# Two sparse layers of a two-layer block, the dense work between them done per token tile beside the row fetches

## The chip, the cores and the metric

One NeuronCore of a Trainium2 chip runs the whole program. The metric is the device time of one execution in microseconds (us). The kernel before takes 3065.58 us, the median of 3 runs (3065.04 to 3068.65). All data is fp32.

## What is computed

256 tokens with 1024 features go through two blocks. The first (pooling and windowed attention, a 32-expert layer, a gated embedding) is left alone. The second has two layers. Layer 0 begins with a recurrent unit, layer 1 with stick-breaking attention; each then has a sparse feed-forward layer (PEER) and a gated embedding (PLE). The part that matters:

```python
def peer_ffn(h, w_q, sub_keys, u_tab, v_tab):      # 8 heads, top 16 of 128x128 experts each
    q = xt @ w_q                                   # [T, 8, 2, 128]
    s = einsum('thpd,hpnd->thpn', q, sub_keys)     # 128 scores per half
    sv, si = top_k(s, 16); cand = sv[0][:, None] + sv[1][None, :]
    cv, ci = top_k(cand, 16)                       # 128 experts (eidx) per token
    act = gelu(einsum('cd,ckd->ck', x, u_tab[eidx]))
    return einsum('ck,ckd->cd', softmax(cv) * act, v_tab[eidx])

def per_layer_embed(h, p, g, w_gate, w_proj):
    return h + sigmoid(rms_norm(h, g) @ w_gate) * (p @ w_proj)

# layer 1, attention: k and v from rms_norm(h, kv_norm), q from rms_norm(h, norm_mix), 16 heads of 64
z = q k^T / 8;  A = exp(log_sigmoid(z) + suffix sum over keys of (log_sigmoid(z) - z)), causal
h = h + (A v) @ w_o
```

A query looks at earlier tokens only, so tile 0 (tokens 0 to 127) needs nothing of tile 1. All other steps of the second block after layer 0's recurrent unit are per token. At the end there is one more root-mean-square norm.

## The kernel before, in words

Activations lie feature-major: `xT`, `hT` and `mT` hold for each of 8 feature chunks 128 partitions x 256 tokens. Weights stream on SP's queue through `ring`, 8 slots of 128x1024 (0.524 MB); `load` (L312) waits until the slot's last user is done, and `plan` fixes the order of all chunks. `dense` (L417) takes a chunk's 128x128 blocks as stationary weights and streams 256 tokens; `token_major` (L430) does v the other way round. fp32 matmuls are issued as two instructions each.

`peer` (L711 on PE, L1008 on ACT, L1425 on DVE, L1578 on POOL) runs once per layer. Norm and queries come first, for both tiles. A **unit** is one head of one tile, 16 picks; there are 16 units, 256 **picks** per layer. A pick fetches for each of the 128 tokens of a tile one row of 8 KB, u and v joined, by an indirect DMA of POOL (L1587) into one of `ROWS` = 16 buffers in `big`. DVE then multiplies u with the tokens and sums (L1477), ACT takes gelu (L1031) of a **share** of 4 picks, DVE makes the coefficients (L1484), ACT scales an identity matrix by each (L1039, `DIAGS` = 8 buffers), and PE multiplies this diagonal with v, two halves of 512 columns, into two PSUM banks (L739). That frees the row buffer. DVE finds the expert numbers of unit n+2 in four pieces, one after each share's dots of unit n (`choose`, L1497). So each engine has its order written out by hand:

```python
for n in range(UNITS):
    for g in range(SHARES):
        share_dots(n, g)
        ...
        if n + 2 < UNITS:
            choose(n + 2, g)
        share_coef(n, g)
```

After layer 0's last pick the outputs are transposed and added to `xT` (L750, L1493). Then for both tiles together: `ple` (L675), k (L424), v (L437), q (L424), attention in groups of four heads (L779 to L813; POOL masks the weights at L1597), the output product, and layer 1's norm and queries. Only then does POOL get the first index of layer 1. Layer 1 ends with `ple` and the final norm; one DMA writes the output (L399).

Of the kernel before, what the change touches and what calls it, by code (L numbers as in the profile page):

```python
# [31 lines left out]
P = 128  # L32
T = 256
# [29 lines left out]
ROWS = 16  # L63
# [3 lines left out]
SHARE = 4  # L67
SHARES = PTOP // SHARE
DIAGS = 8
BIG = ROWS * ROW  # L70

# [38 lines left out]
def plan():  # L110

    first, n = {}, 0
    for name, chunks in (
        ("w_in", 16), ("w_pool", 1), ("w_out", 8), ("w_router", 1), ("b_down", 1), ("proj0", 2), ("ple0", 8),
        ("a_x", 8), ("a_y0", 3), ("w_r", 1), ("a_y1", 1), ("w_i", 1), ("a_y2", 4), ("a_out", 8),
        ("wqa0", 8), ("wqb0", 2), ("keysa0", 1), ("wqc0", 6), ("keysb0", 1), ("proj1", 2), ("ple1", 8),
        ("kv", 16), ("bq", 8), ("bo", 8),
        ("wqa1", 8), ("wqb1", 2), ("keysa1", 1), ("wqc1", 6), ("keysb1", 1), ("proj2", 2), ("ple2", 8),
    ):
        first[name] = n  # L120
        n += chunks
    return first

# [28 lines left out]
def program(nc, io, out):  # L152
    first = plan()
    with ExitStack() as ctx:
# [35 lines left out]
        def half(bank, e):  # L190
# [19 lines left out]
            "diags_ready rows_used out_copied out_turned "  # L210
            "q2_ready k2_ready v2_ready z_done z_used spm_ready rc_done arg_ready a_exp w_exp a_ready o_done o_ready "
# [55 lines left out]
        k2, q2, v2 = lru[0], lru[1], lru[2]  # L267
        st = [big[:, 3 * W + k * SPAN:3 * W + (k + 1) * SPAN] for k in range(28)]
# [22 lines left out]
        def tok_bank(tt):  # L291

            return (2, 0)[tt]

        def out_bank(tt):

            return (6, 4)[tt]
# [9 lines left out]
        def _(sync):  # L307
# [76 lines left out]
            for L in range(2):  # L384
                w, keys = io["peer_w_q"][L], io["sub_keys"][L]
                dense(f"wqa{L}", w)
                for c in range(2):
                    load(first[f"wqb{L}"] + c, w[c * P:(c + 1) * P, SLOT:2 * SLOT])
                load(first[f"keysa{L}"], keys[:, 0:SLOT])
                for c in range(2, DT):  # L390
                    load(first[f"wqc{L}"] + c - 2, w[c * P:(c + 1) * P, SLOT:2 * SLOT])
                load(first[f"keysb{L}"], keys[:, SLOT:2 * SLOT])
                ple(L + 1, io["p2"][L], io["ple_w_proj"][L], io["ple_w_gate"][L])
                if L == 0:
                    dense("kv", io["w_kv"], 2)
                    dense("bq", io["b_w_q"])
                    dense("bo", io["b_w_o"])
            sync.wait_ge(S["out_ready"], 8)
            sync.dma_start(out, mT[:, :]).then_inc(S["out_stored"], 16)  # L399
            sync.wait_ge(S["out_stored"], 16)  # L400
# [3 lines left out]
        def _(pe):  # L404
# [24 lines left out]

            def token_major(n, src, ready, at, cols, outs):  # L430

                for c in range(DT):
                    pe.wait_ge(ready, at + c + 1)
                    w = chunk(n + c)
                    for tt in range(TT):
                        for k, o in enumerate(outs[tt]):
                            last = pe.matmul(o, tile(src, c)[:, tt * P:(tt + 1) * P],  # L437
                                             w[:, cols + k * BANK:cols + (k + 1) * BANK],
                                             start=(c == 0), stop=(c == DT - 1), skip_group_check=True)
                    last.then_inc(w_used, 1)  # L440
# [270 lines left out]
            def peer(L, norm, at):  # L711
                sum_squares(norm)
                dense(first[f"wqa{L}"], hsrc, 0, h_ready, at)
                dense(first[f"wqb{L}"], hsrc, 4, cs=range(0, 2))

                def scores(z):
# [941 lines left out]
```

## Time and profile before

| | |
|---|---|
| median of 3 runs | 3065.58 us |
| profiled execution | 3064.01 us, its span 3062.2 us |
| TensorE (PE) busy, mean granted clock | 2637.0 us (86%), 0.937 |
| VectorE (DVE) busy | 1343.3 us (44%) |
| ScalarE (ACT) busy | 544.5 us (18%) |
| GpSimd (POOL) busy | 509.5 us (17%) |
| moved by DMA | 1025.92 MB, mean 335 GB/s |
| of that, indirect row fetches | 540.05 MB |

The span runs from the first to the last instruction. Busy times of engines overlap. A slice of the page is a fortieth of the span, 76.6 us. Layer 0's picks are in slices 19 to 27, the dense part between the layers in 27 to 31, layer 1's picks from 31 to 40. Which engine sets the pace of a stretch is read from who waits for whom there.

### The profile page before, as it was taken

Reading aid. Unit: us, or ns where it says so; the run is one execution under the profiler, and the core shown is the slowest. Engines: PE = TensorE matmul, PEld = TensorE weight load, DVE = VectorE, ACT = ScalarE, POOL = GpSimd, SP = SyncE. Lnnn points to the kernel's source line nnn. Section 1 sums busy time; section 2 is a strip of 40 time slices with the busy share of each in tenths; the row PEclk is TensorE's granted clock in tenths of the full one; section 3 lists DMA queues with packets and bytes.
Section 4 is the critical chain, followed back from the end, with each engine's and each line's share of the span. In section 5 each row is a group of like instructions: output and inputs, shape, how many; then the busy total and the mean of one; then the engine's idle time right before and its main releaser. Section 6 shows DMA issues by size and latency. Waiting matters only on the chain.

```text
span 3062.2 us, 29257 instructions
## 1 busy us (share of the span) xinstructions
PE 2637.0 (86%) x10044; PEld 1391.2 (45%) x10044; DVE 1343.3 (44%) x3484; ACT 544.5 (18%) x1283; POOL 509.5 (17%) x556
## 2 busy tenths in 40 slices
PE   8789999999999998997778777789888778787787
PEld 6554444444443436784333333347677333333335
DVE  2222221212212223416777777641234777777752
ACT  0210010000101002202222222211331222122212
POOL 1000000000000000004333333300012333333320
PEclk9779999999999998998998999999889898989999
DMA  6259999999999993349999999953216999999990
GB/s 216 94 208 417 417 419 417 418 417 418 418 417 419 417 406 113 128 137 393 421 421 422 421 421 421 421 231 123 90 61 256 422 421 421 422 421 422 421 420 34
DMA packets 169837, 1025.92 MB, mean 335 GB/s; under 512 B 17488, under 2 KB 17904, under 8 KB 71184
## 3 DMA queue, kind: packets, MB, share of 16 engines
q0 software_dynamic: 74880, 540.05, 42.5%
q1 hardware_dynamic: 94864, 484.73, 40.1%
q8 instruction: 46, 0.75, 0.1%
q14 instruction: 47, 0.39, 0.0%
HBM read 1022.09 MB, written 2.62 MB: 335 GB/s over the span
## 4 chain that ended last, share of the span: by engine, by line
PE 44%; DMA 36%; DVE 8%; SPq 7%; issue 2%; ACT 2%; POOL 1%; DVEq 0%; ACTq 0%; POOLq 0%
DMA big<-in_uv,small 28%; PE ps L424 12%; PE ps L569 11%; PE ps L739 9%; DMA big<-in_w_gate_up 7%; SPq L342 4%; PE ps L559 3%; SPq L334 2%; PE ps L604 1%; DVE big L1477 1%; PE ps L414 1%; PE ps L437 1%; POOL big L1587 1%; PE ps L683 1%; DMA big<-in_w_down 1%
## 5 line engine op out<-in xcount | busy, mean ns | idle before, releaser
L739 PE MATMUL ps<-big,small 128*128 128x512 f32 x2048 | 1008.1, 650 | 283.8 <-ACT small L1039 283.8
L1587 POOL DMA_INDIRECT big<-in_uv,small x512 | 484.1, 946 | 2174.4 <-DVE small L1466 1406.6
L739 PEld LDWEIGHTS ps<-big,small 128*128 128x128 f32 x2048 | 415.2, 208 | 872.7 <-issue 492.9
L1477 DVE SCALAR_TENSOR_TENSOR big<-big,ps 128x1024 f32<-128x1024 f32 x512 | 617.6, 1219 | 349.6 <-DMA big<-in_uv,small 347.9
L569 PE MATMUL ps<-big 128*64 128x512 f32 x3072 | 705.8, 600 | 24.2 <-DMA big<-in_w_gate_up 21.6
L569 PEld LDWEIGHTS ps<-big 128*64 128x64 f32 x3072 | 202.9, 137 | 421.6 <-issue 333.9
L424 PE MATMUL ps<-hT,ring 128*128 128x256 f32 x1408 | 317.4, 388 | 14.5 <-DVE hT L1126 11.5
L424 PEld LDWEIGHTS ps<-hT,ring 128*128 128x128 f32 x1408 | 272.9, 195 | 58.6 <-DVE hT L1126 13.1
L1039 ACT ACTIVATE small<-con,small 128x128 f32<-128x128 f32 x512 | 163.6, 390 | 293.1 <-DVE small L1484 293.1
L1303 DVE COPY big<-ps 128x512 f32<-128x512 f32 x32 | 22.1, 692 | 426.1 <-PE ps L569 426.1
L1289 DVE TENSOR_TENSOR big<-ps,big 128x256 f32<-128x256 f32 x64 | 27.2, 425 | 308.2 <-PE ps L586 308.2
L1031 ACT ACTIVATE small<-small 128x4 f32<-128x4 f32 x128 | 26.3, 205 | 694.6 <-DVE big L1477 694.6
L559 PEld LDWEIGHTS ps<-small,mT 128*128 128x128 f32 x1024 | 120.0, 196 | 26.6 <-issue 26.6
L559 PE MATMUL ps<-small,mT 128*128 128x64 f32 x1024 | 124.4, 281 | 1.0 <-DVE small L1273 1.0
L424 PE MATMUL ps<-mT,ring 128*128 128x256 f32 x512 | 113.1, 383 | 5.2 <-issue 3.1
L424 PEld LDWEIGHTS ps<-mT,ring 128*128 128x128 f32 x512 | 98.2, 192 | 20.3 <-issue 3.9
L941 ACT COPY big<-ps 128x512 f32<-128x512 f32 x32 | 18.7, 585 | 421.0 <-PE ps L569 421.0
L414 PE MATMUL ps<-mT,con 128*128 128x256 f32 x176 | 48.4, 431 | 25.2 <-ACT mT L845 25.2
L604 PE MATMUL ps<-small,big 64*128 64x256 f32 x512 | 65.4, 396 | 2.4 <-ACT small L928 2.4
L933 ACT ACTIVATE big<-big 128x256 f32<-128x256 f32 x64 | 26.7, 417 | 225.6 <-DVE big L1290 225.6
L604 PEld LDWEIGHTS ps<-small,big 64*128 64x128 f32 x512 | 48.3, 191 | 31.5 <-issue 27.1
L414 PEld LDWEIGHTS ps<-mT,con 128*128 128x128 f32 x176 | 37.2, 218 | 35.5 <-ACT mT L845 21.9
(246 smaller groups left out, 1633.2 us busy)
## 6 DMA issues: line engine op xcount, KB each, us to landing
big<-in_w_gate_up SPq DMA_DIRECT2D x256, 1024.0 KB, 20.5
big<-in_w_down SPq DMA_DIRECT2D x128, 1024.0 KB, 24.2
ring<-in_peer_w_q SPq DMA_DIRECT2D x32, 512.0 KB, 3.7
ring<-in_w_in SPq DMA_DIRECT2D x16, 512.0 KB, 5.2
ring<-in_a_w_in SPq DMA_DIRECT2D x16, 512.0 KB, 3.6
ring<-in_ple_w_gate SPq DMA_DIRECT2D x16, 512.0 KB, 5.9
big<-in_uv,small POOLq DMA_INDIRECT x512, 26.3
ring<-in_w_kv SPq DMA_DIRECT2D x16, 512.0 KB, 3.7
```

The source lines that it names most:

```text
L334: sync.dma_start(moe_slot(k), io["w_gate_up"][e, k * P:(k + 1) * P, :]).then_inc(moe_loaded[k], 16)
L342: sync.dma_start(moe_slot(GU_CHUNKS + k).rearrange("p (s d) -> p s d", s=2), src)\
L414: last = pe.matmul(ps[:, 7, 0:T], ones, tile(mT, c), start=(c == 0), stop=(c == DT - 1))
L424: last = pe.matmul(half(bank, e), w[:, e * P:(e + 1) * P], src(c), start=(c == 0 and e % 2 == 0), stop=(c == DT - 1), skip_group_check=True)
L437: last = pe.matmul(o, tile(src, c)[:, tt * P:(tt + 1) * P], w[:, cols + k * BANK:cols + (k + 1) * BANK], start=(c == 0), stop=(c == DT - 1 ...
L559: last = pe.matmul(ps[:, G_X, c * CAP:(c + 1) * CAP], mT[:, tt * D + c * P:tt * D + (c + 1) * P], m_sel[:, tt * CAP:(tt + 1) * CAP], start ...
L569: last = pe.matmul(ps[side * CAP:(side + 1) * CAP, bank + b, :], o, w[:, at:at + BANK], start=start, stop=stop, skip_group_check=True)
L604: last = pe.matmul(half(G_OUT, side * DT // 2 + c), m_y[at, c * P:(c + 1) * P], m_gateT[at, :], start=False, stop=True, skip_group_check=True)
L739: last = pe.matmul(ps[:, out_bank(tt) + z, :], diagonal(k), rows(k)[:, D + z * BANK:D + (z + 1) * BANK], start=(k % (PH * PTOP) == 0), sto ...
L1039: act.activation(diagonal(k), ident, ACT.Copy, scale=coef[:, k:k + 1])\
L1477: ins = dve.scalar_tensor_tensor(u, u, 1.0, tok, op0=ALU.mult, op1=ALU.mult, accum_out=dots[:, k:k + 1])
L1587: pool.indirect_dma_start(out=rows(k), out_offset=None, in_=io[f"uv{L}"], in_offset=bass.IndirectOffsetOnAxis(ap=rows_at[:, k:k + 1], axis ...
```

## The change

`ROWS` goes from 16 to 10, `SHARE` from 4 to 2. The 512 picks of both layers become one sequence of 4 **phases** of 128 picks (layer 0 tile 0, layer 0 tile 1, layer 1 tile 0, layer 1 tile 1), and a phase has 64 **ticks** of 2 picks. **Chain** q is what follows phase q's picks for that one tile. Chains 0 and 1 hold PLE, k, v, q, attention, output product, and layer 1's queries and scores; chains 2 and 3 hold PLE and the final norm. In each tick of phase f every engine first does its share of the picks and then one step of chain f-1. Chain 3 runs after the last pick, in 9 ticks. The steps sit at fixed ticks:

```diff
-ROWS = 16
+ROWS = 10
-SHARE = 4
+SHARE = 2
+PHASES = 2 * TT
+PHASE = PH * PTOP
+TICKS = PHASE // SHARE
+ADD, PROJ, SQUARE, SCALE, TURN, GAIN, GATE, SIGMOID, GATED = 0, 0, 0, 1, 1, 2, 2, 6, 7
+SQUARE2, SCALE2, TURN2, GAIN2 = 7, 8, 8, 9
+KEY, VALUE, KEY_COPY, KEY_TURN, KEY_KEEP, VALUE_KEEP = 9, 13, 13, 14, 15, 17
+QUERY, QUERY_COPY, QUERY_TURN, QUERY_KEEP = 17, 21, 21, 22
+HEADS, GROUP, GROUPS = 22, 3, HEADS2 // 4
+MERGE, ADD3, SQUARE3, SCALE3, TURN3, GAIN3 = 34, 38, 38, 39, 39, 40
+ASK, ASK_COPY, SCORE, SCORE_KEEP = (40, 44), (44, 48), (44, 48), (45, 49)
+TOKENS, CHOOSE = 49, 46
+TAIL_TICKS = 9
```

The dense products (GATE, KEY, VALUE, QUERY, MERGE, ASK) take 4 ticks each, 2 chunks a tick. The order on PE, and DVE's tick:

```diff
+            for f in range(1, PHASES):
+                if f >= 2:
+                    pe.wait_ge(S["scores_kept"], 4 + 4 * (f - 1))
+                for t in range(TICKS):
+                    picks(f, t)
+                    chain(f - 1, t)
+            for t in range(TAIL_TICKS):
+                chain(3, t)
...
+            def share(f, t):
+                n = f * TICKS + t
...
+                for which, piece in chosen(f, t):
+                    choose(which, piece)
+                at = slice(n * SHARE % PICKS, n * SHARE % PICKS + SHARE)
+                dve.wait_ge(S["gelu_ready"], n + 1)
+                dve.scalar_tensor_tensor(coef[:, at], acts[:, at], p_rec[:, u16:u16 + 1], cv[:, at],
+                                         op0=ALU.mult, op1=ALU.mult).then_inc(S["coef_ready"], 1)
```

In phase 0 a piece of `choose` runs in every second tick, two units ahead. In later phases the phase's own last six units are chosen in ticks 0 to 40, and the next phase's first two units in ticks 46 to 53.

The chain keeps the residual token-major (`xk`, in place of `hT`). A dense product of one tile has the tile's features as stationary operand and streams the weights in two halves of 512 columns; only the queries keep the old form, with 128 tokens streamed. A root-mean-square is one ACT instruction with an accumulator, then a root; the scaled tile is transposed on PE and multiplied by the gain on ACT and DVE:

```diff
+                def stationary(seg, src, bank, cs, begin=0):
+                    for c in cs:
+                        w = chunk(first[f"{seg}{q}"] + begin + c)
+                        for z in range(2):
+                            last = pe.matmul(ps[:, bank + z, :], src[:, blocks(c)], w[:, z * BANK:(z + 1) * BANK],
+                                             start=(c == 0), stop=(c == DT - 1), skip_group_check=True)
+                        last.then_inc(w_used, 1)
...
+                            for e in range(DT):
+                                last = pe.matmul(ps[:, A + e // 4, blocks(e % 4)], w[:, blocks(e)], hd[:, blocks(c)],
+                                                 start=(c == 0 and e % 4 == 0), stop=(c == DT - 1), skip_group_check=True)
+                            last.then_inc(w_used, 1)
```

In the attention a group of four heads takes 3 ticks, on operands of 512 columns in chain 0 and 1024 in chain 1. ACT and DVE (the masks moved from POOL to DVE):

```diff
+                    if t == HEADS + GROUP * g + 1:
+                        act.wait_ge(S["z_done"], no + 1)
...
+                        step.link(act.activation(sides(a_buf, cols), pair(bank, cols), ACT.Abs))
+                        step.link(act.activation(a, a, ACT.Exp, scale=-1.0))
+                        act.activation(a, a, ACT.Ln, bias=1.0).then_inc(S["ln_ready"], 1)
+                    if t == HEADS + GROUP * g + 3:
+                        act.wait_ge(S["arg_ready"], no + 1)
+                        act.activation(w_buf[:, 0:cols], w_buf[:, 0:cols], ACT.Exp).then_inc(S["w_exp"], 1)
...
+                    if t == HEADS + GROUP * g + 4:
+                        dve.wait_ge(S["w_exp"], no + 1)
+                        dve.tensor_tensor(heads(w_buf), heads(w_buf), mask2, ALU.mult).then_inc(S["a_ready"], 1)
```

SP loads the weights of every chain anew, POOL fetches in one loop, and the output leaves in four pieces:

```diff
+            for q in range(TT):
+                ple_chain(q)
+                dense(f"kv{q}", io["w_kv"], 2)
+                dense(f"bq{q}", io["b_w_q"])
+                dense(f"bo{q}", io["b_w_o"])
+                for z in range(2):
+                    for c in range(DT):
+                        load(first[f"ask{z}_{q}"] + c, w[c * P:(c + 1) * P, z * SLOT:(z + 1) * SLOT])
+                    load(first[f"keys{z}_{q}"], keys[:, z * SLOT:(z + 1) * SLOT])
+            sync.wait_ge(w_used, first["bq1"] + 8)
+            sync.dma_start(hd2, io["final_row"].partition_broadcast(P)).then_inc(S["gain_loaded"], 16)
+            for tt in range(TT):
+                ple_chain(TT + tt)
+                for z in range(2):
+                    sync.wait_ge(S["out_ready"], 2 * tt + z + 1)
...
+            for n in range(2 * UNITS):
+                pool.wait_ge(S["idx_ready"], n + 1)
+                for k in range(n * PTOP, (n + 1) * PTOP):
+                    if k >= ROWS:
+                        pool.wait_ge(S["rows_used"], k + 1 - ROWS)
```

## Rows read from the trace of the kernel before

**Rows 1.** The page's second part, 40 slices: DMA busy tenths, then GB/s.

```profile
DMA  6259999999999993349999999953216999999990
GB/s 216 94 208 417 417 419 417 418 417 418 418 417 419 417 406 113 128 137 393 421 421 422 421 421 421 421 231 123 90 61 256 422 421 421 422 421 422 421 420 34
```

**Rows 2.** The page's chain that ended last, its shares by line.

```profile
DMA big<-in_uv,small 28%; PE ps L424 12%; PE ps L569 11%; PE ps L739 9%; DMA big<-in_w_gate_up 7%; SPq L342 4%; PE ps L559 3%; SPq L334 2%; PE ps L604 1%; DVE big L1477 1%; PE ps L414 1%; PE ps L437 1%; POOL big L1587 1%; PE ps L683 1%; DMA big<-in_w_down 1%
```

**Rows 3.** Windows: busy us of each engine, granted PE clock, DMA share, GB/s.

```profile
1700.00:2000.00 300.00, 232.95 (x487) 96.95 (x486) 212.81 (x533) 66.35 (x180) 113.27 (x120) 0.92 1.01 421
2046.00:2339.00 293.00, 264.69 (x1193) 216.48 (x1194) 70.98 (x156) 70.93 (x128) 12.13 (x16) 0.92 0.30 100
2100.00:2186.00 86.00, 84.04 (x317) 61.24 (x315) 6.41 (x14) 3.98 (x8) 0.00 (x0) 0.98 0.43 143
2186.00:2253.00 67.00, 52.06 (x289) 43.97 (x289) 31.84 (x64) 47.38 (x90) 12.13 (x16) 0.77 0.01 5
3003.00:3062.00 59.00, 44.15 (x201) 36.90 (x200) 16.56 (x28) 12.64 (x19) 0.00 (x0) 0.95 0.10 36
```

**Rows 4.** Waits, 1410 to 2000 us: us in total, times, longest.

```profile
POOL big L1587 <- PE ps L739: 371.3, 232, 8.4
...
DVE big L1477 <- DMA big<-in_uv,small: 149.9, 136, 2.7
...
PE ps L739 <- ACT small L1039: 126.7, 52, 5.5
...
DVE small L1484 <- ACT small L1031: 3.8, 5, 2.7
```

**Rows 5.** Line 1587, the row fetches: count and first issue; us from issue to landing.

```profile
L1587 POOL DMA_INDIRECT big<-in_uv,small x512: 932/936/1167, 1382.3 to 2965.6; - x171
...
DMA to landing us min/median/max: 8.3/26.3/33.2
```

**Rows 6.** Chain that ended last, pieces in order: start us, us, what.

```profile
2006.19 30.02 DMA big<-in_uv,small
2036.24 1.24 DVE big L1477 x2
2038.46 7.15 PE ps L739 x16
...
2128.95 27.47 PE ps L437 x64
...
2325.14 3.58 PE ps L722 x32
```

**Rows 7.** The page's sixth part: a load of weights by itself.

```profile
ring<-in_peer_w_q SPq DMA_DIRECT2D x32, 512.0 KB, 3.7
```

**Rows 8.** DMA, 1368 to 1402 us: weight loads beside the first row fetches.

```profile
ring<-in_ple_w_gate SPq DMA_DIRECT2D x6, 512.0 KB, 8.7
```

**Rows 9.** Lines: busy us, mean ns of one; idle before it, releaser.

```profile
L1477 DVE SCALAR_TENSOR_TENSOR big<-big,ps 128x1024 f32<-128x1024 f32 x512 | 617.6, 1219 | 349.6 <-DMA big<-in_uv,small 347.9 <-PE ps L730 1.7
...
L1039 ACT ACTIVATE small<-con,small 128x128 f32<-128x128 f32 x512 | 163.6, 390 | 293.1 <-DVE small L1484 293.1
...
L1031 ACT ACT_TABLE_LOAD x30 | 38.5, 1283 | 0.5
...
L1264 DVE TENSOR_SCALAR small<-small 128x128 f32<-128x128 f32 x64 | 15.4, 283 | 4.7 <-DVE small L1257 4.6
...
L1085 ACT ACTIVATE big<-big 128x384 f32<-128x384 f32 x16 | 8.4, 523 | 0.5
...
L1013 ACT COPY big<-ps 128x512 f32<-128x512 f32 x16 | 8.2, 600 | 103.1 <-PE ps L424 103.1
...
L1132 DVE TENSOR_TENSOR xT<-ps,xT 128x512 f32<-128x512 f32 x12 | 7.5, 683 | 87.9 <-PE ps L424 87.9
```

**Rows 10.** Timeline at the end: start us, us, the output's issue.

```profile
3057.88 0.35 SPq L399 DMA_DIRECT2D out<-mT  x1
```

More of the change, by code:

```diff
@@ L398, in _ @@
-            sync.wait_ge(S["out_ready"], 8)
-            sync.dma_start(out, mT[:, :]).then_inc(S["out_stored"], 16)
-            sync.wait_ge(S["out_stored"], 16)
+            w, keys = io["peer_w_q"][0], io["sub_keys"][0]
+            dense("wqa", w)
+            for c in range(2):
+                load(first["wqb"] + c, w[c * P:(c + 1) * P, SLOT:2 * SLOT])
+            load(first["keysa"], keys[:, 0:SLOT])
+            for c in range(2, DT):
+                load(first["wqc"] + c - 2, w[c * P:(c + 1) * P, SLOT:2 * SLOT])
@@ L428, in dense @@
                         between(c)
[L430 to L440, printed above, removed]
             hsrc = lambda c: tile(hT, c)
@@ new lines, in queries, with keep, exps @@
+            def queries(z):
+                for b in range(4):
+                    act.copy(pq[:, (4 * z + b) * BANK:(4 * z + b + 1) * BANK], ps[:, 4 * z + b, :])\
+                        .then_inc(S["pq_ready"], 1)
+            def keep(z):
+                used_through(act, f"keys{'ab'[z]}", 1)
+                for b in range(2):
+                    act.copy(tile(mT, 2 * z + b, BANK), ps[:, 4 * z + 2 + b, :]).then_inc(S["scores_kept"], 1)
+            def exps(n):
+                act.wait_ge(S["cv_ready"], n + 1)
+                u = n % UNITS
+                e = cv[:, u * PTOP:(u + 1) * PTOP]
+                act.activation(e, e, ACT.Exp, bias=p_nmax[:, u:u + 1], accum_out=p_sum[:, u:u + 1])\
+                    .then_inc(S["cv_exp"], 1)
@@ new lines, in _ @@
+            squares(5)
+            used_through(act, "wqa", 8)
+            queries(0)
+            keep(0)
+            used_through(act, "wqc", 6)
+            queries(1)
+            keep(1)
+            exps(0)
+            exps(1)
+            for f in range(PHASES):
+                for t in range(TICKS):
+                    share(f, t)
+                    for n, piece in chosen(f, t):
+                        if piece == 3:
+                            exps(n)
+                    if f == 0 and t in (6 * SHARES + 1, 7 * SHARES + 1):
+                        tt = t // SHARES - 6
+                        act.wait_ge(S["x_turned"], tt + 1)
+                        for z in range(2):
+                            act.copy(xk[:, tt * D + z * BANK:tt * D + (z + 1) * BANK], ps[:, 4 + z, :])\
+                                .then_inc(S["x_kept"], 1)
+                    if f:
+                        chain(f - 1, t)
@@ L1116, in _ @@
+            for t in range(TAIL_TICKS):
+                chain(3, t)
         @block.vector
@@ L1565, in _ @@
+            norm(5, [("norm_ffn", 0)])
+            for n in range(2):
+                for piece in range(4):
+                    choose(n, piece)
+            for f in range(PHASES):
+                for t in range(TICKS):
+                    share(f, t)
+                    if f:
+                        chain(f - 1, t)
+            for t in range(TAIL_TICKS):
+                chain(3, t)
         @block.gpsimd
```

792 lines of the change are left out of this document (436 added, 356 removed).

## The prediction, made before the changed kernel was run

> **What bounds the kernel now.** I read the page first. The DMA share is 9 tenths over most of the span and falls in four places; two lie around the change, slices 27 to 30 and the very end [rows 1]. The chain that ended last gives 28% of the span to the row fetches [rows 2]. The windows say how. While rows are fetched the 16 DMA engines are full at 421 GB/s, with TensorE (PE) busy 233 of 300 us, VectorE (DVE) 213, ScalarE (ACT) 66; in the 293 us between the two sparse layers they move 100 GB/s and PE is busy 265 us [rows 3]. The waits confirm it: DVE waits for rows and PE for the diagonals that follow from them, while DVE hardly waits for ACT [rows 4]. So the fetches are DMA-bound, the part between is PE-bound, and they never overlap. That is what the change can win; the question is what it pays.
>
> **One row fetch** is 128x8 KB = 1.049 MB, at 421 GB/s 2.49 us. Test: the first issue is at 1382.3 us, the last landing of layer 0 at 2036.2, 653.9 us [rows 5, 6]. The shortest landing, 8.3, plus 256x2.49 = 637.4, plus some 6 weight chunks of 0.524 MB at 1.25 us (7.5), is 653.2. The model holds, and I use it for the change. The Trainium skill ("DMA: Bandwidth & Descriptors", Where 436 GB/s comes from) puts the HBM limit of a core near 358 GB/s; the row at 421 contradicts it, and I go by the row. By the page the added weights below would cost about 30 us more.
>
> **The sum, DMA first.** After the change there are 512 fetches in an unbroken stream: 1274.9 us. Between them run the weights: chain 0 and chain 1 load 60 chunks each (2 projection, 8 gate, 16 key/value, 8 query, 8 output, 16 next queries, 2 keys), chains 2 and 3 load 10 each, and 2 are in before the first fetch: 138x1.25 = 172 us. What was loaded once in the gap, where no rows moved, is now loaded twice and between rows: the price is 172 us for a gap of 293. Gain vector and output are 1 MB, 2 us. With 8.3 at the start the last row lands, if DMA never pauses, at 1382.3+8.3+1274.9+172+2 = 2839.5. Phase 0 is thereby some 320 us, phases 1 and 2 395 each (319+75), phase 3 332.
>
> **PE beside it.** Picks: 233/300 of 319 = 248 us a phase. Chain of one tile: a token-stationary 1024x1024 product was 27.47 us for both tiles, so 13.7 for one [rows 6]. Gate, k, v, q, output are five: 68.5. The next queries keep weights stationary over 128 columns, 256 instructions at 3.58/32 = 0.112 us: 28.6. Scores 3.6, projection 3.4, six transposes of 8 instructions 5.4. Attention was 52 us busy at clock 0.77 for both tiles [rows 3], so 40 at full speed, 20 a tile (less for the first, more for the second). Sum 130: 378 of 395 us. PE stays just under DMA.
>
> **DVE.** 213/300 of 319 = 227. The halved share adds 32 gelu/coefficient steps of 0.4: 13. Chain: ten 512-column operations at 0.69, three scalings at no more than the 1.22 of a dot product over 1024 columns, 16 gains of 128 columns at 0.28, attention 32/2 = 16, and the masks that leave POOL, about 4: 35 us [rows 3, 9]. 275 of 395. **ACT:** 71 + 32x0.2 + attention 47/2, some 24 copies and gains (14), three root-mean-squares at 4 us, and 20 table loads in the attention at 1.28 (26): about 155 [rows 3, 9]. **POOL** loses the masks, keeps its fetches, and no longer waits for them; its order is otherwise the same. **SP** now has the final gain vector and the first tile's output in its queue, ahead of the last chain's weights; those are needed only 60 ticks later, nothing.
>
> **Fewer buffers.** 26.3 us to landing is 10.6 fetches in flight, so 5.4 of 16 were held by compute [rows 5]. With shares of 2 they are held shorter, about 4 of 10, 6 in flight; 8.3/2.49 = 3.3 are enough. Zero; it costs from the point where over 6.7 are held.
>
> **Where ticks are longer than their DMA.** A tick is 2 picks, 5 us of DMA, 7.5 where 2 chunks come along. Dense tick: PE 3.6+3.4 = 7.0, inside. Attention, three ticks a group, 15 us: ACT has 3 gelus and 6 diagonals (3.0), 5 table loads (6.4), and four operations that are 0.52 us at 384 columns, so some 0.6 at 512 (first tile) and 1.0 at 1024 (second), plus a copy: 12 and 14 us. It hands over in line to DVE (argument, mask, coefficients), 5 to 6 us: 17 and 20. Four groups lose 8 and 20, and the top-16 pieces that DVE runs there another 5 for the second tile; 8 chunks are prefetched meanwhile, 10 us of DMA work, so 0 and 15 are left. Table switches around the three root-mean-squares hold DVE about 2 us each, 14 in all, half of it taken up by the buffers: 7. PE at 96% of DMA in order queues a little: 4 us per phase, 8. **Stalls 30 us.** The trace shows no such interleaving, so the bounds: nothing is lost (0); or PE keeps all the idle time that it has beside rows now (67 of 300 us), so that chain work adds to 319 us: 319+130 = 449, 54 more than 395 twice, plus 15 in phase 3: 123. I take 30, near the low end, because what stands idle now waits for rows, not for a neighbour [rows 4].
>
> **Tail.** After the last landing, two dots, gelu, two diagonals and 8 matmuls: 7 us (9.4 before). Then before it was 59 us for both tiles [rows 3]. Now for one: add 1.4, square and root with table 3.2, scale 1.2, transposes and gains 2.4, gate 13.7, sigmoid 1.2, product and sum 2.8, square and root 3.0, final scaling 1.6, output 4.3 [rows 10], hand-overs 1.2: 36.
>
> Span: 2839.5+30+7+36 = 2912.5 against 3062.2. The profiled execution is 1.8 longer than its span, and 1.6 shorter than the median: **2915 us** in terms of the median, 4.9% less.
>
> **Rivals.**
> A. *All stalls are hidden*: the buffers and the prefetched chunks swallow them. For: in the rows DVE waits 150 us for DMA, so there is room. Against: PE at 96%. Gives 2885.
> B. *PE becomes the bound.* Its granted clock in the rows is 0.92 on average, between its levels of 1.2 and 2.4 GHz, against 0.98 in the dense part, since it stands between bursts [rows 3]. If it keeps the gaps as well as the slow stretches: 123 us instead of 30, 3008. If instead the chain fills the gaps and the clock is full, PE needs 228+130 = 358 and the forecast has more room. The Trainium skill ("TensorE: Matmul & The Clock Gate", Whether your matmuls stay warm) sides with the second: activity releases the clock. The trace agrees as far as 0.98 where PE is busy 84 of 86 us; no row shows the mix.
> C. *Ten buffers are too few.* Weight chunks beside row fetches land after 8.7 us instead of 3.7 [rows 7, 8], so the queues share the engines, and row latency rises too. If 7 are held, 3 are in flight, 8.3/3 = 2.77 us a row, 0.28x512 = 143 more: 3058, no change. Against: 4.6 in flight would do even at today's holding.
> D. *Slower: lockstep.* In a chain tick DVE's dots, ACT's gelu, DVE's coefficients, ACT's diagonals, PE's picks and chunks come one after another, and the next tick starts only when a chain wait (keys turned, weights used, spm, arguments) is over, because each engine's program is in order. Serial, a dense tick is 2.3+1.3+0.4+0.8+7.0 = 11.8 instead of 7.5, an attention or hand-over tick 3 more than 5: 2x(28x4.3+22x3) = 373 us, 3258. It decides from 178 us, 1.8 us per tick over 100 ticks. Against: eight diagonals let ACT run four ticks ahead, and chain steps are mostly put one tick after what they need.
> That the overlap isn't there at all is excluded: the picks of the next phase stand between the chain steps in every engine's order.
>
> **Chances.** Forecast 0.50, A 0.18, B 0.17, C 0.07, D 0.08. The range reaches from A, with rounding, to just under B's end: 2882 to 2995; outside are D, C's worst and B's. A measurement of this kernel can tell about 0.2% (6 us) from no change. Faster: all but D and a sliver of C, 0.91; within 0.2%: 0.01; slower 0.08.
>
> **What would show it.** DMA share 9 or 10 tenths from 1400 to 2840 us without a gap; last row landing near 2870; phases 0 to 3 of 320, 400, 415 and 335 us; PE busy over 90% in phases 1 and 2 with its clock above 0.95; landing of a row near 15 us instead of 26; tail near 36. Right by DMA is also seen in the waits: POOL for PE rare, DVE for rows frequent. Wrong: in phases 1 and 2 a DMA share under 0.9 with POOL waiting for PE and DVE or PE waiting for ACT (D; B if PE itself is full), or a landing at 8 us with few rows in flight (C).

## The result, and the profile after

The changed kernel takes 2917.36 us (median of 4 runs, 2910.07 to 2925.10) against 3066.23 before: ratio 0.9509, 95% interval 0.9491 to 0.9527. Forecast were 2915 us and a range of 2882 to 2995. The profiled execution below is the slowest of the four, 2925.1 us with a span of 2923.1.

Of the page after: busy times, and the 40 slices of 73.1 us with PE's granted clock, DMA's share and GB/s; below them the shares by line of the chain that ended last.

```profile
PE 2575.4 (88%) x9916; PEld 1293.1 (44%) x9916; DVE 1343.3 (46%) x3589; ACT 654.1 (22%) x1471; POOL 496.8 (17%) x540
...
PEclk9679999999999999999998999999999999999999
DMA  6159999999999998234999999999999989999994
GB/s 209 50 209 407 419 417 418 418 417 418 417 418 418 418 418 354 94 130 136 398 421 421 421 421 418 418 371 408 420 419 417 397 332 394 421 406 421 421 422 195
...
DMA big<-in_uv,small 16%; PE ps L950 15%; PE ps L631 11%; DMA big<-in_w_gate_up 8%; PE ps L498 7%; PE ps L784 4%; SPq L388 3%; SPq L396 3%; PE ps L621 3%; DVE big L1673 3%; PE ps L901 2%; PE ps L666 1%; ACT small L1274 1%; ACT L1269 1%
```

The hole of [rows 1] is gone: from slice 20 on DMA is full, with dips in slices 27, 28, 32 to 34 and 36 (332 GB/s at the lowest). The row fetches have shrunk from 28% [rows 2] to 16% of the chain, and the picks (L950) stand beside them with 15%. Both limits now share the stretch.

Windows of the changed kernel, cut at the first pick of each phase (columns as in rows 3):

```profile
1415.00:1732.00 317.00, 255.26 (x537) 106.33 (x538) 240.85 (x641) 84.16 (x230) 120.13 (x127) 0.91 1.01 419
1732.00:2135.00 403.00, 355.66 (x1097) 174.33 (x1096) 262.60 (x690) 143.34 (x313) 121.45 (x129) 0.97 1.01 408
2135.00:2557.00 422.00, 367.38 (x1193) 185.03 (x1192) 265.69 (x689) 150.28 (x313) 120.34 (x128) 0.97 0.98 396
2557.00:2889.00 332.00, 268.25 (x560) 108.69 (x561) 224.71 (x562) 87.53 (x231) 111.76 (x118) 0.94 0.98 407
```

From the first pick of a phase to that of the next the trace gives 316.2, 402.9, 422.3 and 332.6 us; the prediction named 320, 400, 415 and 335. DMA works at 419 GB/s in phase 0 and loses rate in phase 2 above all.

Four windows within phase 2: ticks 9 to 21 (k, v and q products), 22 to 33 (attention groups), 34 to 40, and 52 to 62 (the quiet end).

```profile
2193.00:2284.00 91.00, 88.03 (x218) 39.50 (x216) 55.50 (x154) 22.33 (x60) 24.86 (x27) 1.00 1.02 417
2284.00:2375.00 91.00, 69.41 (x255) 36.45 (x256) 58.64 (x138) 56.27 (x83) 22.50 (x24) 0.89 0.89 345
2375.00:2427.00 52.00, 46.10 (x147) 22.83 (x146) 35.82 (x93) 17.95 (x40) 13.12 (x14) 0.97 0.95 375
2496.00:2550.00 54.00, 40.70 (x88) 15.81 (x88) 32.01 (x68) 12.70 (x37) 20.87 (x22) 1.00 1.01 422
```

In the dense ticks DMA and PE are full at once. In the attention 12 ticks take 91 us; DMA could move their rows in 60, falls to 345 GB/s, and loses (421-345)/421 x 91 = 16 us, and 6 more in the third window. At the quiet end it is DMA alone that sets 4.9 us a tick; the same ticks take 3.8 us where no rows are fetched (e3 below).

Waits in phase 2 (us in total, times, longest):

```profile
POOL big L1810 <- PE ps L950: 299.9, 127, 8.7
...
DVE big L1673 <- DMA big<-in_uv,small: 61.6, 44, 2.6
...
PE ps L950 <- ACT small L1274: 57.5, 28, 6.2
DVE small L1684 <- ACT small L1269: 54.6, 37, 15.9
...
DVE big L1764 <- PE ps L871: 10.9, 4, 3.9
```

Against [rows 4] (590 us there, 422 here) DVE waits less for rows, and much more for ACT's gelu: 54.6 us instead of 3.8. Not all of that lies in the attention. Two waits of the 54.6 us, 22.7 together, are in ticks 44 and 48, where gelu stands behind an ACT copy of the next queries that itself waits for PE; DMA loses only 2 us in ticks 41 to 48 (405 GB/s in 56 us). The waits from 2440 to 2483 us:

```profile
DVE small L1684 <- ACT small L1269: 22.7, 2, 15.9
ACT big L1238 <- PE ps L901: 27.3, 2, 16.2
```

The chain at the end (start us, us, what):

```profile
2864.93 18.56 DMA big<-in_uv,small
...
2885.72 3.71 PE ps L950 x8
...
2889.53 1.30 DVE hT L1700 x2
...
2897.07 15.69 PE ps L784 x32
```

The last row is on its way for 18.6 us, not the 30.0 of [rows 6], with 10 fetches out at most instead of 16. It lands at 2883.5; PE ends 5.9 us later, and the tail takes 33.7.

### The profile page after: what moved, and what is told of

The parts are those of the page before. It is cut to its first block, busy times and chain, and to the rows that moved or that the text cites. A ratio compares the mean times of both kernels' runs of the same rounds, so it can differ in the third digit from the quotient of the medians.

```text
span 2923.1 us, 29391 instructions
## 1 busy us (share of the span) xinstructions
PE 2575.4 (88%) x9916; PEld 1293.1 (44%) x9916; DVE 1343.3 (46%) x3589; ACT 654.1 (22%) x1471; POOL 496.8 (17%) x540
## 4 chain that ended last, share of the span: by engine, by line
PE 50%; DMA 25%; DVE 10%; SPq 7%; ACT 4%; issue 2%; another core or an unknown queue 1%; POOL 0%; DVEq 0%; ACTq 0%; POOLq 0%
DMA big<-in_uv,small 16%; PE ps L950 15%; PE ps L631 11%; DMA big<-in_w_gate_up 8%; PE ps L498 7%; PE ps L784 4%; SPq L388 3%; SPq L396 3%; PE ps L621 3%; DVE big L1673 3%; PE ps L901 2%; PE ps L666 1%; ACT small L1274 1%; ACT L1269 1%
## 5 line engine op out<-in xcount | busy, mean ns | idle before, releaser
L950 PE MATMUL ps<-big,small 128*128 128x512 f32 x2048 | 991.3, 634 | 232.5 <-ACT small L1274 231.5
L950 PEld LDWEIGHTS ps<-big,small 128*128 128x128 f32 x2048 | 398.8, 202 | 780.6 <-issue 446.1
L1274 ACT ACTIVATE small<-con,small 128x128 f32<-128x128 f32 x512 | 178.6, 396 | 315.8 <-DVE small L1684 313.9
L498 PE MATMUL ps<-hT,ring 128*128 128x256 f32 x768 | 176.8, 392 | 8.8 <-DVE hT L1314 5.8
L1269 ACT ACTIVATE small<-small 128x2 f32<-128x2 f32 x256 | 52.7, 206 | 535.7 <-DVE big L1673 532.0
L498 PEld LDWEIGHTS ps<-hT,ring 128*128 128x128 f32 x768 | 150.5, 197 | 35.3 <-issue 7.2
L784 PE MATMUL ps<-ring,xT 128*128 128x512 f32 x320 | 145.1, 598 | 1.3 <-ACT xT L1175 1.3
L1684 DVE SCALAR_TENSOR_TENSOR small<-small 128x2 f32<-128x2 f32 x256 | 56.0, 219 | 152.5 <-ACT small L1269 150.5
L1088 ACT COPY big<-ps 128x512 f32<-128x512 f32 x32 | 18.8, 587 | 421.3 <-PE ps L631 421.3
L784 PEld LDWEIGHTS ps<-ring,xT 128*128 128x128 f32 x320 | 61.3, 192 | 78.7 <-issue 77.2
L901 PEld LDWEIGHTS ps<-xT,ring 128*128 128x128 f32 x512 | 59.5, 192 | 7.0 <-issue 6.7
```

What stands on the lines that cost most here:

```text
L498: last = pe.matmul(half(bank, e), w[:, e * P:(e + 1) * P], src(c), start=(c == 0 and e % 2 == 0), stop=(c == DT - 1), skip_group_check=True)
L784: last = pe.matmul(ps[:, bank + z, :], src[:, blocks(c)], w[:, z * BANK:(z + 1) * BANK], start=(c == 0), stop=(c == DT - 1), skip_group_ch ...
L901: last = pe.matmul(ps[:, A + e // 4, blocks(e % 4)], w[:, blocks(e)], hd[:, blocks(c)], start=(c == 0 and e % 4 == 0), stop=(c == DT - 1), ...
L950: last = pe.matmul(ps[:, out_bank(f) + z, :], diagonal(k), rows(k)[:, D + z * BANK:D + (z + 1) * BANK], start=(k % PHASE == 0), stop=((k + ...
L1269: act.activation(acts[:, at], dots[:, at], ACT.Gelu_apprx_tanh).then_inc(S["gelu_ready"], 1)
L1274: act.activation(diagonal(k), ident, ACT.Copy, scale=coef[:, k % PICKS:k % PICKS + 1])\
```

## The experiments

All are edits of the changed kernel. The three sets of runs had medians of 3066.7, 3068.1 and 3067.0 us for the kernel before, so totals can be laid side by side. Profiled executions differ in one thing that no edit touches: the first fetch is issued anywhere from 1375.5 (e2) to 1386.9 us (the changed kernel), as these rows of the fetch line show (e2, then the changed kernel):

```profile
L1826 POOL DMA_INDIRECT big<-in_uv,small x512: 932/936/1404, 1375.5 to 2877.3; - x171
```

```profile
L1810 POOL DMA_INDIRECT big<-in_uv,small x512: 932/936/1408, 1386.9 to 2864.9; - x171
```

So the lengths of the phases, each from its first pick on PE to the next phase's, tell more than totals. Two executions of the changed kernel (the first and the last row below) agree within 1.0 us in each phase, and phases 0 and 3, which e4, e5, e7, e9 and e10 leave alone, vary by up to 1.5 us, so a difference of one or two us in a phase shows nothing.

| kernel | median us | ratio to before, 95% | phases 0 to 3, us |
|---|---|---|---|
| changed | 2917.36 | 0.9509 (0.9491 to 0.9527) | 316.2, 402.9, 422.3, 332.6 |
| e1 less PE | 2910.60 | 0.9492 (0.9472 to 0.9512) | 315.2, 400.3, 417.7, 334.1 |
| e2 more DMA | 2944.75 | 0.9603 (0.9583 to 0.9622) | 314.8, 421.5, 428.4, 333.5 |
| e3 no rows | 2807.03 | 0.9155 (0.9135 to 0.9175) | 314.6, 380.4, 399.5, 272.4 |
| e4 no tables | 2905.31 | 0.9471 (0.9454 to 0.9489) | 314.7, 401.0, 410.4, 332.9 |
| e5 groups of 4 ticks | 2925.07 | 0.9536 (0.9508 to 0.9564) | 315.6, 406.7, 427.5, 333.3 |
| e6 early pieces | 2918.52 | 0.9523 (0.9494 to 0.9551) | 314.8, 401.5, 417.8, 334.0 |
| e7 merged exponentials | 2929.34 | 0.9547 (0.9519 to 0.9574) | 316.1, 409.6, 428.2, 333.3 |
| e8 8 buffers | 2932.93 | 0.9563 (0.9536 to 0.9590) | 320.8, 409.2, 425.9, 336.8 |
| e9 = e7, argument later | 2913.29 | 0.9490 (0.9467 to 0.9514) | 314.8, 403.7, 415.4, 333.1 |
| e10 lagged steps | 2912.14 | 0.9496 (0.9477 to 0.9516) | 314.7, 404.3, 416.0, 333.1 |
| e11 lagged, early pieces | 2904.21 | 0.9463 (0.9443 to 0.9484) | 315.7, 399.8, 409.5, 333.1 |
| e12 changed, again | 2918.54 | 0.9513 (0.9495 to 0.9532) | 316.0, 403.1, 421.3, 333.4 |

The theory: DMA sets the length, with stalls in the attention ticks. The first rival: PE sets it.

### e1: less work for PE

```diff
-                        for z in range(2):
+                        for z in range(1 if 0 < c < DT - 1 else 2):
                             last = pe.matmul(ps[:, bank + z, :], src[:, blocks(c)], w[:, z * BANK:(z + 1) * BANK],
```

> Leaves out the second 512-column half of 6 of the 8 chunks in the gate, k, v, q and output products of the chains (the results are then not the reference's); every load stays. That takes 6x0.857 = 5.1 us of PE work out of each product, 26 us out of chains 0 and 1 each, 5 out of chains 2 and 3. Theory (DMA sets phases 1 and 2, with stalls in the attention ticks): dense ticks no longer take PE's 6.9 us but what DMA gives, the total falls by 0 to 15 us from 2917, and the DMA share stays full. Rival (PE is the bound, since every dense tick takes exactly PE's 6.9 us): the total falls by 50 to 60 us, to about 2862.

Phases 1 and 2 lost 2.6 and 4.6 us of the 26 us of PE work that each gave up, the total 7. PE isn't the bound, though its 6.9 us stood in every dense tick. Part of the 7 is the tail, whose gate product is shorter. Ticks 9 to 21, where most of the work was taken out, kept their length (91 to 94 us, DMA at 417 GB/s, PE busy 77 of 92 us instead of 88 of 91). The gain lies in ticks 34 to 40, the output product: 45 us instead of 52 in phase 2. Ticks 41 to 48 weren't touched by this edit. There PE does set the pace: it is busy all 56 us, with rows and, in e3, without them, and DMA stays at 405 GB/s.

```profile
2186.00:2278.00 92.00, 76.79 (x187) 33.96 (x186) 55.67 (x154) 22.78 (x62) 25.27 (x27) 0.96 1.02 417
...
2368.00:2413.00 45.00, 40.85 (x133) 20.18 (x132) 33.86 (x88) 16.88 (x37) 13.45 (x14) 0.96 0.99 393
```

### e2: more work for DMA

```diff
+            def spare():
+                if spares[0]:
+                    sync.wait_ge(S["spare_loaded"], 16 * spares[0])
+                sync.dma_start(at(11 * D, D), io["b_w_q"][0:P, :]).then_inc(S["spare_loaded"], 16)
+                spares[0] += 1
...
+                        if c % 2:
+                            spare()
```

> Adds one spare load of 0.524 MB, into columns that nobody reads, after every second chunk of the k, v, q and output weights: 16 in each of chains 0 and 1, 32x1.25 = 40 us of DMA work. Theory (DMA-bound): 30 to 40 us longer, 2947 to 2957. Rival (PE-bound, DMA has slack): at most 10 us longer.

27.4 us more, just under the 30 to 40. The phases tell why: phase 1 takes 18.6 of its 20 us (403 to 421.5), phase 2 only 6.1. Phase 1 is DMA-bound up to what it had idle itself; phase 2 had 22 us of idle DMA in ticks 22 to 40, and 14 of the added 20 didn't show in its length. The trace shows where they went: the spare loads hold back SP's queue, 11 chunks come in during the attention ticks instead of 2, and DMA works at 394 GB/s there instead of 345, in no more time:

```profile
2302.00:2390.00 88.00, 69.76 (x257) 36.61 (x256) 57.45 (x137) 55.64 (x81) 22.80 (x25) 0.90 0.97 394
```

### e3: no rows

```diff
-                    dve.wait_ge(rows_loaded[k % ROWS], 16 * (k // ROWS + 1))
+                    dve.wait_ge(rows_loaded[k % ROWS], 16 * (min(k, PHASE + ROWS - 1 - (PHASE + ROWS - 1 - k) % ROWS) // ROWS + 1))
-                    ins = dve.scalar_tensor_tensor(r, r, 1.0, tok,
+                    ins = dve.scalar_tensor_tensor(r, r, 1.0 if k < PHASE else 0.0, tok,
...
-                for k in range(n * PTOP, (n + 1) * PTOP):
+                for k in range(n * PTOP, min((n + 1) * PTOP, PHASE + ROWS)):
```

> From the 11th pick of phase 1 on no row is fetched any more; the picks work on the rows that lie in the ten buffers, with a factor 0 in the dot product (its results are then not the reference's). All compute and all weights stay. Theory: what is left is the order of the engines; phases 1 and 2 fall to PE's busy time plus some waits, 360 to 375 and 375 to 395 us, phase 3 to 240 to 280, the total to 2740 to 2800. Rival (the engines' order already sets phases 1 and 2): these two keep 400 and 420 within 10 us and only phase 3 gets shorter.

Phases 1 to 3 of this kernel:

```profile
1718.00:2099.00 381.00, 351.73 (x1097) 174.80 (x1098) 257.19 (x689) 143.24 (x315) 0.71 (x1) 0.98 0.29 96
2099.00:2498.00 399.00, 366.63 (x1192) 186.65 (x1191) 261.89 (x688) 149.73 (x313) 0.00 (x0) 0.96 0.25 81
2498.00:2770.00 272.00, 249.63 (x561) 105.98 (x560) 218.69 (x563) 87.60 (x231) 0.00 (x0) 0.97 0.06 22
```

With DMA at a quarter of its share the engines' order still takes 380.4 and 399.5 us, 5 us over what the theory allowed (and the total 7). That is the number which changed my view: DMA alone would need 395 (the prediction's byte count), the order alone 380 and 399.5, both together take 403 and 422. In phase 2 the order by itself is longer than DMA by itself. They don't simply give the larger of the two, because they alternate: in attention ticks 22 to 33 the order takes 87.6 us here and 91 with rows, while at the end, ticks 49 to 63, it takes 58.1 against 73.9 with rows.

### e4: no table functions in the attention

```diff
-                        step.link(act.activation(a, a, ACT.Exp, scale=-1.0))
-                        act.activation(a, a, ACT.Ln, bias=1.0).then_inc(S["ln_ready"], 1)
+                        step.link(act.activation(a, a, ACT.Copy, scale=-1.0))
+                        act.activation(a, a, ACT.Copy, scale=1.0).then_inc(S["ln_ready"], 1)
...
-                        act.activation(w_buf[:, 0:cols], w_buf[:, 0:cols], ACT.Exp).then_inc(S["w_exp"], 1)
+                        act.activation(w_buf[:, 0:cols], w_buf[:, 0:cols], ACT.Copy).then_inc(S["w_exp"], 1)
```

> In the chains' attention the exponentials and the logarithm are plain copies (the results are then not the reference's), so that ACT reloads no function table there: 5x1.28 us less per group, 26 us less of ACT per chain, of which the attention ticks of chain 1 (120 us for 16 ticks, DMA at 353 GB/s) were to suffer most. Theory (stalls come from ACT's tables and hand-overs): phase 1 loses 5 to 10 us, phase 2 15 to 25, total 2885 to 2900. Rival (those ticks are long by PE's or DVE's own work or by the top-16 pieces): under 5 us in all.

Phase 2 lost 12 us, phase 1 two, which is hardly more than two executions differ. Both are under the theory's ranges, the total of 2905 is over its 2900, and the rival (under 5 us in all) misses too. The edit took away 18 loads per chain (24 are left of 42, by the traces), not 20, so 23 us of loads cost 12 and 2: they are half of the stall in chain 1 and nearly free in chain 0.

### e5: the same steps, spread over more ticks

```diff
-HEADS, GROUP, GROUPS = 22, 3, HEADS2 // 4
-MERGE, ADD3, SQUARE3, SCALE3, TURN3, GAIN3 = 34, 38, 38, 39, 39, 40
+HEADS, GROUP, GROUPS = 22, 4, HEADS2 // 4
+MERGE, ADD3, SQUARE3, SCALE3, TURN3, GAIN3 = 37, 41, 41, 42, 42, 43
```

> A group of four heads takes 4 ticks instead of 3; the output product and all that follows moves 3 ticks later. No instruction is added or taken away. The run without row fetches showed that the engines' order alone needs 380 and 399 us for phases 1 and 2, DMA alone 395, and both together took 403 and 422. Theory: in the attention ticks of chain 1 the order is slower than 5 us of DMA, so work there should be spread over more ticks, which the quiet end of the phase (3.4 us of engines against 5 of DMA) has to spare: phase 2 loses 10 to 20 us, phase 1 0 to 8, total 2893 to 2907. Rival (the sum of the engines' order counts, wherever it stands): no change within 5 us of 2917.

Both phases got longer, by 3.8 and 5.2 us. The theory of density fell, and so did its rival by a little. Ticks 22 to 33 of phase 2 took 91.2 us with three groups in them, as they had with four. So a tick there isn't long by the number of its steps alone. One thing works against the edit and wasn't tested apart: PE's granted clock was 0.83 there instead of 0.89, and 213 matmuls kept PE busy as long (69.9 us) as 255 had (69.4).

```profile
2279.00:2371.00 92.00, 69.89 (x213) 34.43 (x214) 56.93 (x137) 48.04 (x75) 22.92 (x24) 0.83 0.88 335
```

This led to the hand-overs. Timeline of the changed kernel around one of them, from the first group of chain 1 (start us, us, engine, line; in brackets the idle time and who ended it):

```profile
2302.27 3.27 PE L950 MATMUL ps<-big,small 128*128 128x512 f32 x6
...
2304.58 0.70 ACT L1274 ACTIVATE small<-con,small 128x128 f32<-128x128 f32 x2 [0.29 <-DVE small L1684]
...
2305.38 0.59 PE L866 MATMUL ps<-big,con 128*128 128x256 f32 x2
...
2307.54 0.59 PE L871 MATMUL ps<-big,con 128*128 128x256 f32 x2
2307.97 3.60 PE L950 MATMUL ps<-big,small 128*128 128x512 f32 x8
2308.17 1.23 DVE L1764 TENSOR_TENSOR big<-ps,big 128x1024 f32<-128x1024 f32 x1 [3.62 <-PE ps L871]
2309.31 1.21 DVE L1673 SCALAR_TENSOR_TENSOR big<-big,ps 128x1024 f32<-128x1024 f32 x1
2309.43 1.06 ACT L1225 ACTIVATE big<-big 128x1024 f32<-128x1024 f32 x1 [2.85 <-DVE big L1764]
```

PE does two picks first, then the suffix products (L866 to L871). DVE, which runs about a tick ahead of PE, stands 3.6 us in front of its argument (L1764), with the dots of the next tick behind it, and ACT stands 2.9 us behind DVE, with the next gelu behind it. The step is at the tick after PE's, which isn't far enough.

### e6: pieces early

```diff
-    now = [(PH * f + 2 + j // 4, j % 4) for j in range(24) if int(1.75 * j) == t]
+    now = [(PH * f + 2 + j // 4, j % 4) for j in range(24) if j == t]
```

> The 24 pieces of finding expert numbers run in ticks 0 to 23 of phases 1 to 3 instead of being spread to tick 40, so that 14 of the attention ticks' DVE steps have none beside them. Theory (a piece of 1.6 to 3.9 us on DVE lies in the hand-over chain of the attention ticks): phase 2 loses 5 to 10 us, phase 1 up to 5, phase 3 nothing, total 2903 to 2912. Rival (pieces lie in DVE's shadow while ACT works; early they disturb the hand-overs of ticks 0 to 9): no change or up to 5 us longer.

Unclear by the total (2918.5 against 2917.4). In its profiled execution phases 1 and 2 lost 1.4 and 4.5 us. Taken alone it settles nothing; e11 below tries the same edit again.

### e7: merged exponentials

```diff
-                    if t == HEADS + GROUP * g + 3:
+                    if t == HEADS + GROUP * g + 4:
                         act.wait_ge(S["arg_ready"], no + 1)
```

Mask and output product move from tick 4 to 5 of the group, the copy from 5 to 6.

> The exponential of the attention weights moves one tick later, next to the exponential of the following group's logits, and mask, output and copy follow one tick later each; 8 table loads of 1.28 us less per chain. The run with no tables at all lost 12 us for 20 loads a chain less. Theory: a good third of that, 4 to 8 us, total 2909 to 2913. Rival (only the load in front of gelu holds DVE, and the merged tick gets longer by what the other saves): no change.

Wrong both ways: 6.7 and 5.9 us longer, though ACT does less (36 table loads a chain instead of 42; the expectation said 8 fewer). The next experiment shows where it went.

### e8: 8 row buffers

```diff
-ROWS = 10
+ROWS = 8
```

> 8 row buffers instead of 10. Theory (about 4 rows are held by compute and 3.3 fetches in flight are enough): phases 0 and 3 keep their length within 3 us, phases 1 and 2, whose ticks of 7 to 9 us hold more, lose 3 to 8 each, total 2920 to 2935. Rival C of the prediction (ten are at the edge): 2.77 us a row or more in all phases, over 60 us longer.

2932.9, inside the theory's 2920 to 2935; rival C falls. Phases 0 and 3 lost 4.6 and 4.2 us instead of at most 3, phases 1 and 2 6.3 and 3.6. Two buffers are worth 16 us in all: a slope, no cliff.

### e9: e7 with the argument one tick later

```diff
-                    if t == HEADS + GROUP * g + 3:
+                    if t == HEADS + GROUP * g + 4:
                         dve.wait_ge(S["rc_done"], no + 1)
```

> The merged-exponential kernel (e7) with one more step moved: DVE takes the argument (suffix sum minus softplus) one tick later, when PE's suffix products of the tick before have long run. In the traces DVE stands there for up to 5 us, since PE does the picks of the tick first and only then the suffix products. Theory (a chain step that waits for a step placed at most one tick before holds the dots of the next tick): phases 1 and 2 lose 5 to 12 us each against e7's 410 and 428. Rival (that wait only takes the place of a wait for rows or gelu): within 3 us of e7.

Against e7 phase 1 lost 5.9 us, phase 2 12.8, the total 16. DVE's wait for PE at this step and the attention window, each time e7 and then e9:

```profile
DVE big L1764 <- PE ps L871: 14.9, 4, 5.0
...
2285.00:2414.00 129.00, 101.17 (x337) 50.44 (x338) 76.35 (x188) 54.69 (x92) 30.58 (x32) 0.88 0.85 329
```

```profile
DVE big L1764 <- PE ps L871: 0.4, 1, 0.4
...
2281.00:2397.00 116.00, 98.08 (x337) 49.29 (x338) 76.28 (x188) 54.76 (x92) 30.23 (x32) 0.93 0.94 367
```

The same instructions, 129 us and 116 us. The wait was four times up to 5 us, and without it the window is 13 us shorter. 3 of the 13 are in PE's own busy time (101 and 98 us, at a granted clock of 0.88 and 0.93). The 13 us are measured against e7, which was slower than the changed kernel; why the merging by itself made it slower isn't shown, beyond DVE's wait here of 14.9 us instead of 10.9. Against that, run again beside it (e12), e9 took 2913.29 us (2907.34 to 2916.16) and not 2918.54 (2917.62 to 2920.49): 5 us, by the merged loads and the later argument together, and by phases 6 in phase 2 and nothing in phase 1.

### e10 and e11: every step behind what it needs

```diff
-HEADS, GROUP, GROUPS = 22, 3, HEADS2 // 4
+HEADS, GROUP, GROUPS = 22, 4, HEADS2 // 4
...
-                    if t == HEADS + GROUP * g + 3:
+                    if t == HEADS + GROUP * g + 4:
                         dve.wait_ge(S["rc_done"], no + 1)
...
-                    if t == HEADS + GROUP * g + 3:
+                    if t == HEADS + GROUP * g + 5:
                         act.wait_ge(S["arg_ready"], no + 1)
```

> Groups of 4 ticks, as in e5, and in them every step at least one tick, DVE's argument two ticks, behind what it needs: argument at 4, exponential at 5 (beside the next group's, one table load shared), mask and output product at 6, copy at 7; the rest of the chain 4 ticks later than in the changed kernel. Nothing is added. Theory (hand-overs within a tick are what makes the attention ticks long): phase 2 405 to 415 instead of 422, phase 1 397 to 403, total 2895 to 2910, and DMA in the attention ticks of chain 1 above 380 GB/s instead of 345. Rival (the instructions' own sum counts): 2917 to 2925, like e5.

> e10 with the pieces of e6 in ticks 0 to 23. Theory: both act on the same ticks and add up in part: phase 2 400 to 410, phase 1 396 to 401, the sum of the phases 15 to 30 us under the changed kernel's 1474. Rival: as e6 alone, 6 us less.

> The changed kernel, once more, on the same chip and in the same rounds as e10 and e11, so that these are compared with it directly. Expected: 2917 within 8 us, phases of 316, 403, 422 and 333 us within 3.

e10: phase 2 took 416.0, phase 1 404.3; each misses its range by 1 us, the total its range by 2, and DMA in the attention reached 364 GB/s, not 380. Against e5, with groups as long, the phases lost 2.4 and 11.5 us; but e10 also merges table loads, as e9 does, and against e9 nothing is gained (403.7 and 415.4 there, 404.3 and 416.0 here). Longer groups with every step lagged are thus not shown to be better than the one step that e9 moves. e11 adds the pieces: 399.8 and 409.5. Against e10 that is the only difference, and it is worth 8 us: 2904.21 (2898.05 to 2905.79) and 2912.14 (2908.70 to 2916.49), ranges that don't touch. That settles e6: the pieces on DVE do cost time in the attention ticks. Its four phases sum to 1458.1 us, 15.7 less than e12's 1473.8, at the low end of 15 to 30. e12 itself took 2918.54 us with phases as expected, all within 1 us. The attention windows of e12 (16 ticks) and e11 (20 ticks):

```profile
2280.00:2400.00 120.00, 98.72 (x337) 49.65 (x337) 76.50 (x188) 61.91 (x97) 29.98 (x32) 0.91 0.91 353
```

```profile
2280.00:2408.00 128.00, 111.27 (x368) 54.96 (x369) 68.15 (x131) 55.64 (x100) 37.46 (x40) 0.95 0.95 368
```

Both windows hold the attention and the output product; e11's holds 8 picks more, 20 us of DMA, in 8 us more. In direct comparison e11 took 2904.21 us (2898.05 to 2905.79) and e12 2918.54 (2917.62 to 2920.49): the ranges don't touch, 14 us or 0.5%. e11 leaves nothing out of the computation, and it is the fastest version.

## Why the prediction was right, point by point

**The total.** The span of the profiled execution was 2923.1 us, the sum had 2912.5. The difference adds up: 4.6 us by a later first fetch, 9.4 by more stalls, less 1.1 and 2.3 in the tail. That the median (2917.36) lies only 2.4 us from the forecast is partly luck, as the profiled execution was 7.7 us above the median. The rounding helped too: 2912.5+1.8+1.6 is 2915.9.

**Bound and byte model.** Right. 1386.9+8.3+1274.9+172+2 = 2844.1 for an unbroken DMA; the last row landed at 2883.5, so 39 us of stalls against 30 forecast. The first fetch came 4.6 us later than before, of which 3.7 us arose in the first weight loads of the program, long before the change. e2 agrees with 1.25 us a chunk where DMA is the bound: 16 chunks cost phase 1 18.6 us, 1.16 each. The 421 GB/s held, and 417 to 418 beside weight loads, so the Trainium skill's 358 GB/s ("DMA: Bandwidth & Descriptors", Where 436 GB/s comes from) doesn't hold here either.

**PE.** 378 of 395 us forecast, 356 and 367 measured. Two terms were too high. The picks were busy 243 and 244 us (L950), 5 of them together with a chain's matmuls, where I added 248 a phase from the windows before with their clock of 0.92 [rows 3]. And the first tile's attention took PE some 10 us (L853, L866 and L880 in phase 1: 2.9, 4.1 and 2.6), not 20; the second tile's came to about 20. Filled with chain work PE ran at 0.97, in dense ticks at 1.00. The Trainium skill ("TensorE: Matmul & The Clock Gate", What's actually happening) says that activity releases the throttle; the trace agrees, 1.00 where PE is busy 88 of 91 us. Rival B: shown wrong by e1, but for ticks 41 to 48, where PE is busy throughout and DMA loses about 2 us a phase.

**DVE and ACT.** 275 and 155 forecast; 263 to 266 and 143 to 150 measured.

**Fewer buffers at zero.** Half right. With ten buffers DMA stays full where no chain runs (419 GB/s in phase 0), but e8 lost 16 us for two fewer, so the step from 16 wasn't shown to be free; the way back to 16 wasn't tried, as there is no room beside the chain's buffers.

**Attention stalls of 0 and 15 us.** This is the term that was mis-sized. Idle DMA in ticks 22 to 40 was 9 us in chain 0 (381 GB/s in 77 us, 404 in 49) and 22 in chain 1. The step that failed is the credit of 10 us for 8 chunks prefetched meanwhile. SP's queue shows that they were not loaded there, and below it are the row queue and the weight queue from 2284 to 2375 us (packets, MB, share of the 16 engines):

```profile
2255.64 22.64 SPq L368 DMA_DIRECT2D ring<-in_b_w_o  x8
2380.56 23.92 SPq L368 DMA_DIRECT2D ring<-in_peer_w_q  x8
...
q0 software_dynamic: 4132, 30.12, 85.1%
q1 hardware_dynamic: 356, 1.26, 3.5%
```

The output weights follow the queries' chunks into the ring, so all 8 are issued by 2278 us, before the attention at 2284; then no load is issued for 100 us. Between 2284 and 2375 us 1.26 MB of weights came in, 2.4 chunks or 3 us of DMA, not 8 or 10 us. e2 shows from the other side that the credit would have been real: its late chunks did fill those ticks.

Taking the credit away gives 8 and 25, close to the measured 9 and 22, but partly by luck. In chain 1 the 12 ticks took 31 us more than their rows need (91 and 60), where the sum has 25. Row buffers made up for some 12 of the 31: nearly 29 rows were moved there (30.12 MB) for 24 picks, since buffers that were empty after the dense ticks filled up while the picks were late. The sum has no such relief in the attention. And 6 of the 22 us lie behind the attention, in the output product's ticks, where the sum has nothing.

I had the group's length nearly right (20 us forecast, 91/4 = 23 measured) for reasons that were right in part. In chain 1 the tables are worth 12 us (e4) and the pieces, which I had put at 5, 4.5 and 6.5 (phase 2 in e6, and in e11 against e10). The hand-over of the argument, which I had counted as if ACT alone waited, is worth 13 in the form that it has in e7; in the changed kernel's own form, where DVE waits 10.9 us for it, no run took it out alone.

**PE's queueing and the root-mean-squares, 15 us**: not separated by any run. Of the 39 us of stalls 31 lie in ticks 22 to 40, so 8 are left for these two, where the sum has 15; the two misses, 31 for 15 and 8 for 15, partly cancel.

**Tail.** 7+36 forecast, 5.9+33.7 measured.

**Of the signs I named,** three were wrong. The DMA share was not without a gap: it fell to 0.89 in the attention of chain 1, and the last row landed at 2883.5 us instead of near 2870. (Row fetches in the chain took 15.2 to 18.7 us, near the 15 forecast.) PE was over 90% busy in neither phase (88 and 87%), because attention ticks leave it idle. And I wrote that POOL would rarely wait for PE if DMA was the bound; it waited 127 times for 300 us, as in [rows 4]. With all ten buffers given out POOL waits for one to come free whoever is slow: 88 of its 300 us lie between 2275 and 2395 us, where DMA idles, the others where DMA is full. So this wait doesn't tell which side is slow.

**Rivals.** A (nothing stalls, 2885): 39 us did. B and C fell with e1 and e8. D (lockstep) was the right mechanism in the wrong size: hand-overs in order do set the attention ticks, but the stalls in both chains' ticks 22 to 40 come to 31 us where D needed 178 to use up the gain.

## What to carry to other kernels

When a DMA-bound and a compute-bound stage are interleaved, neither full alone sets the time: compare the two limits tick by tick, because buffers bridge only their own depth, and count a prefetch as cover only after looking when its ring slots come free. In engines that run a written-out order, put each hand-over step behind its producer by as many ticks as the consumer runs ahead of it. Here DVE's argument had to stand two ticks behind PE's products and not one: that tick was worth 13 us of phase 2 in the variant with merged exponentials, and 5 us of the total together with the merging, against the changed kernel. Spreading the same work over more ticks made it worse, and moving all other steps back too gained nothing more. Side work on the waiting engine counts as well: finding the expert numbers before the attention ticks was worth 8 us. To test which limit rules, add to the one and take from the other, and read phases instead of totals.

## What the runs showed of the hardware

DMA held 417 to 418 GB/s with 8 KB row fetches and 0.524 MB weight loads mixed, 1% under the 421 for rows alone. The start of the program varied by up to 11 us between executions whose code there is the same, which is as large as most effects studied here. An ACT table load took 1.283 us in every place, and the 18 loads a chain that e4 takes away, 23 us, gave back 2 and 12. PE's clock was lower where PE waits more: in ticks 22 to 33 of phase 2 the granted clock was 0.89 in the changed kernel, 0.85 in e7 and 0.83 in e5, and 1.00 in the dense ticks before them.
